# The recurrence-doubling stage of a fused transformer, mixer and expert kernel: four array quadrants with shared q and X banks, and a regrouped state chain

## The reference, cut to what matters

```
def _rwkv7_scan(r, w, k, v, kh, a):
    def step(state, inp):
        r_t, w_t, k_t, v_t, kh_t, a_t = inp
        removed = jnp.einsum('zhvk,zhk->zhv', state, kh_t)
        state = (state * w_t[:, :, None, :] - removed[..., None] * (kh_t * a_t)[:, :, None, :]
                 + v_t[..., None] * k_t[:, :, None, :])
        return state, jnp.einsum('zhvk,zhk->zhv', state, r_t)
    _, y = lax.scan(step, jnp.zeros((z, h, n, n), jnp.float32), seq)
```

## Time and profile before

| | us |
|---|---|
| median of 3 runs | 3404.02 |
| lowest, highest | 3403.05, 3413.53 |
| profiled execution, span | 3408.2 |
| TensorE busy in it | 3111.3 (91%) |
| the changed stage, first F load used to last chain matmul | about 2203 to 2606 of the span |

### The profile page before, as it was taken

The page is one execution under the profiler, slowest core; times in us unless marked ns, Lnnn a source line. Parts: engine busy times, 40 slices in busy tenths (PEclk is TensorE's granted clock), DMA queues, the critical chain, the costliest instruction groups (busy, mean ns, idle before and its releaser), DMA issues. The chain is left out here.

```text
span 3408.2 us, 53296 instructions
## 1 busy us (share of the span) xinstructions
PE 3111.3 (91%) x21800; PEld 2450.2 (72%) x21800; DVE 1944.8 (57%) x2706; ACT 1276.3 (37%) x1607; POOL 903.3 (27%) x468
## 2 busy tenths in 40 slices
PE   7989999998999979999889998389999869999995
PEld 5467888797777767888678776278886358888883
DVE  3656551201433335553399657775644369999995
ACT  2544331222333333222232223222222247777773
POOL 3023434343222214344312200000100014544530
PEclk9989999999999989999999998699999879999997
DMA  3632222321111112222211100501001149999994
GB/s 141 232 115 111 99 93 92 130 99 74 62 50 62 60 48 91 88 97 99 100 74 61 40 17 1 205 3 52 27 27 79 50 187 359 355 373 368 372 371 189
DMA packets 77469, 439.34 MB, mean 129 GB/s; under 512 B 14944, under 2 KB 18016, under 8 KB 28512
## 3 DMA queue, kind: packets, MB, share of 16 engines
q1 hardware_dynamic: 67776, 427.12, 33.4%
q0 software_dynamic: 9504, 9.47, 0.8%
HBM read 421.85 MB, written 39.85 MB: 135 GB/s over the span
## 5 line engine op out<-in xcount | busy, mean ns | idle before, releaser
L77 POOL TENSOR_TENSOR ring_lo<-ring,unit_hi 128x2048 fp32r<-128x2048 f32 x116 | 536.5, 4626 | 1128.0 <-ACT unit_hi L72 1128.0
L130 PE MATMUL wide<-h_hi,unit_hi 128*128 128x512 f32 x1296 | 516.5, 399 | 45.3 <-DVE h_lo L191 23.9
L132 PE MATMUL wide<-h_hi,ring_lo 128*128 128x512 f32 x1296 | 517.0, 399 | 0.0
L131 PE MATMUL wide<-h_lo,unit_hi 128*128 128x512 f32 x1296 | 516.2, 398 | 0.0
L3112 DVE TENSOR_TENSOR ex_w_lo<-ring,ex_w_hi 128x2048 fp32r<-128x2048 f32 x192 | 437.8, 2289 | 46.5 <-ACT ex_w_hi L3062 45.2
L3062 ACT CAST ex_w_hi<-ring 128x2048 fp32r<-128x2048 f32 x192 | 365.7, 1908 | 115.8 <-DMA ring<-in_weights 107.4
L72 ACT CAST unit_hi<-ring 128x2048 fp32r<-128x2048 f32 x116 | 220.5, 1901 | 419.7 <-PE wide L132 418.2
L130 PEld LDWEIGHTS wide<-h_hi,unit_hi 128*128 128x128 f32 x1296 | 250.0, 193 | 117.1 <-POOL ring_lo L77 18.8
L131 PEld LDWEIGHTS wide<-h_lo,unit_hi 128*128 128x128 f32 x1296 | 245.9, 190 | 53.9 <-issue 0.2
L132 PEld LDWEIGHTS wide<-h_hi,ring_lo 128*128 128x128 f32 x1296 | 245.5, 189 | 52.6
L362 DVE TENSOR_TENSOR ffn_hidden_lo<-ffn_whole,ffn_hidden_hi 128x512 f32 (+1 forms) x44 | 201.0, 4569 | 51.3 <-ACT ffn_hidden_hi L337 51.3
(11 more groups left out here) (522 smaller groups left out, 6114.8 us busy)
## 6 DMA issues: line engine op xcount, KB each, us to landing
ring<-in_weights SPq DMA_DIRECT2D x356, 1024.0 KB, 6.1
factors<-rp_out SPq DMA_DIRECT2D x8, 1536.0 KB, 5.5
rw_F<-factors SPq DMA_DIRECT2D x12, 1024.0 KB, 5.3
tail_both<-pair_rows_out SPq DMA_DIRECT2D x4, 1024.0 KB, 7.9
x<-in_x SPq DMA_DIRECT2D x1, 2048.0 KB, 7.6
x_kept<-x SPq DMA_DIRECT2D x1, 2048.0 KB, 12.2
x<-x_kept SPq DMA_DIRECT2D x1, 2048.0 KB, 8.1
x_mixing<-x SPq DMA_DIRECT2D x1, 2048.0 KB, 7.3
```

Source lines behind the costliest of these rows:

```text
L77: pool.tensor_tensor(self.lo[n % RING][:, :], self.ring[n % RING][:, :], self.hi[n % 2][:, :].bitcast(F32), ALU.subtract).then_inc(self.lo ...
L130: pe.matmul(dst, a[0], b[0], start=start, stop=False)
L131: pe.matmul(dst, a[0], b[1], start=False, stop=False)
L132: return pe.matmul(dst, a[1], b[0], start=False, stop=stop)
```

## The change

Both halves of `rwkv_stage` are edited, and the table of masks.

```diff
-        QB, XB = c.bank[0:2], c.bank[2:4]
+        QB, XB, XTB = c.bank[0], c.bank[1], c.bank[2:4]
...
# starts: the output blocks are swapped between the halves
-                            mm = pe.matmul(side[d][h % 2][half[b], m * DH:(m + 1) * DH], F[d][rows, p % 2, m, 0, half[b]],
+                            mm = pe.matmul(side[d][h % 2][half[1 - b], m * DH:(m + 1) * DH], F[d][rows, p % 2, m, 0, half[b]],
...
# pairs
-                    for part in range(2):
-                        for h in (2 * m, 2 * m + 1):
-                            rows = half[h % 2]
-                            ar = F[d][rows, p % 2, m, 0:2, :].rearrange("p a t -> p (a t)")
-                            mm = pe.matmul(side[d][h % 2][:, 2 * P * part:2 * P * (part + 1)], F[d][rows, p % 2, m, 2 + part, :], ar, start=True, stop=True)
+                    for h in (2 * m, 2 * m + 1):
+                        rows = half[h % 2]
+                        for b in both:
+                            pe.matmul(side[d][h % 2][half[1 - b], 0:P], F[d][rows, p % 2, m, 2, half[b]], F[d][rows, p % 2, m, 0, :], start=True, stop=True)
+                    for h in (2 * m, 2 * m + 1):
+                        rows = half[h % 2]
+                        pe.matmul(side[d][h % 2][:, P:2 * P], F[d][rows, p % 2, m, 2, :], F[d][rows, p % 2, m, 1, :], start=True, stop=True)
+                    for h in (2 * m, 2 * m + 1):
+                        rows = half[h % 2]
+                        ar = F[d][rows, p % 2, m, 0:2, :].rearrange("p a t -> p (a t)")
+                        pe.matmul(side[d][h % 2][:, 2 * P:4 * P], F[d][rows, p % 2, m, 3, :], ar, start=True, stop=True).then_inc(pair_done[d], 1)
...
# q_step
-                    if n >= 1:
-                        pe.wait_ge(q_ready[d], n)
+                    if n + d >= 1:
+                        pe.wait_ge(q_ready[1 - d], n + d)
...
-                                mm = pe.matmul(dst[half[b]], G[d][half[b], p % 2, h, half[b]], X[d][half[b], p % 2, h, :], start=True, stop=True)
+                                mm = pe.matmul(dst[half[b]], G[d][half[1 - b], p % 2, h, half[b]], X[d][half[1 - b], p % 2, h, :], start=True, stop=True)
...
# xx_step; earlier_x counts all X copies of earlier slots, both directions
+                    if k < LAST and earlier_x(p, k, d, g) >= 1:
+                        pe.wait_ge(x_taken, earlier_x(p, k, d, g))
...
-                        x, xt = XB[d][:, e * DH:(e + 1) * DH], XB[d][:, (4 + e) * DH:(5 + e) * DH]
+                        x, xt = XB[:, e * DH:(e + 1) * DH], XTB[d][:, e * DH:(e + 1) * DH]
...
-                                mm = pe.matmul(x[half[b]], XT[d][half[b], p % 2, h, :], Q[d][half[b], h, :], start=True, stop=True)
+                                mm = pe.matmul(x[half[1 - b]], XT[d][half[b], p % 2, h, :], Q[d][half[b], h, :], start=True, stop=True)
...
# chain part 0: state first for even m, values first for odd m (part 3 likewise with "corrected", values and U together)
+                            if m % 2 == 0:
+                                state(True)
+                                values(False)
+                            else:
+                                values(True)
+                                mm = state(False)
...
# chain part 2, U
-                            mm = pe.matmul(side[d][h % 2][:, h // 2 * DH:(h // 2 + 1) * DH], full[d][:, h, :], base[d][:, h, :], start=True, stop=True)
+                            for b in both:
+                                mm = pe.matmul(side[d][h % 2][half[b], h // 2 * DH:(h // 2 + 1) * DH], full[d][:, h, half[b]], base[d][:, h, :],
+                                               start=True, stop=True)
...
# VectorE: masks without the repeated half, reads of the other half in L2368, and a signal after the copy of X
-                                          masks.pair[:, d, :].unsqueeze(1).broadcast_to([P, 2, 2 * P]), ALU.mult).then_inc(pair_masked[d], 1)
+                        dve.tensor_tensor(G[d][:, p % 2, h, :], side[d][h % 2], masks.pair[:, d, :], ALU.mult).then_inc(pair_masked[d], 1)
...
-                                            by_four(XB[d], 0))
+                                            by_four(XB, 0)).then_inc(x_taken, 1)
...
-                masks.pair = r_ctx.enter_context(nc.sbuf_tensor("pair_mask", [P, 2, 2 * P], F32))
+                masks.pair = r_ctx.enter_context(nc.sbuf_tensor("pair_mask", [P, 2, 4 * P], F32))
```

More of the change, by code:

```diff
@@ L2255, in chain, with state, values @@
                             ts = slice(m * P, (m + 1) * P)
-                            for a, rows, hs in heads:
-                                pe.matmul(side[d][0][rows, ts], S[d][rows, m, :], F[d][rows, p % 2, m, 0, :], start=True, stop=False)
-                            for a, rows, hs in heads:
-                                mm = pe.matmul(side[d][0][rows, ts], r.vtm[:, t, hs], G[d][:, p % 2, 2 * m + a, 2 * P:3 * P], start=False, stop=True)
+                            def state(first):
+                                for a, rows, hs in heads:
+                                    mm = pe.matmul(side[d][0][rows, ts], S[d][rows, m, :], F[d][rows, p % 2, m, 0, :], start=first, stop=not first)
+                                return mm
+                            def values(first):
+                                for a, rows, hs in heads:
+                                    mm = pe.matmul(side[d][0][rows, ts], r.vtm[:, t, hs], G[d][:, p % 2, 2 * m + a, 2 * P:3 * P], start=first, stop=not first)
+                                return mm
+                            if m % 2 == 0:
[4 more added lines that the diff above has]
+                                mm = state(False)
                         mm.then_inc(baseT_done[d], 1)
@@ L2279, in chain, with state, corrected @@
                                 ts = slice(m * P, (m + 1) * P)
-                                for a, rows, hs in heads:
-                                    pe.matmul(side[d][0][rows, ts], S[d][rows, m, :], F[d][rows, p % 2, m, 1, :], start=True, stop=False)
-                                for a, rows, hs in heads:
-                                    pe.matmul(side[d][0][rows, ts], U[d][:, place(2 * m + a), :], G[d][:, p % 2, 2 * m + a, P:2 * P],
-                                              start=False, stop=False)
-                                for a, rows, hs in heads:
-                                    mm = pe.matmul(side[d][0][rows, ts], r.vtm[:, t, hs], G[d][:, p % 2, 2 * m + a, 3 * P:4 * P],
-                                                   start=False, stop=True)
+                                def state(first):
+                                    for a, rows, hs in heads:
+                                        mm = pe.matmul(side[d][0][rows, ts], S[d][rows, m, :], F[d][rows, p % 2, m, 1, :], start=first, stop=not first)
+                                    return mm
+                                def corrected(first):
+                                    for a, rows, hs in heads:
+                                        pe.matmul(side[d][0][rows, ts], r.vtm[:, t, hs], G[d][:, p % 2, 2 * m + a, 3 * P:4 * P], start=first, stop=False)
+                                    for a, rows, hs in heads:
+                                        mm = pe.matmul(side[d][0][rows, ts], U[d][:, place(2 * m + a), :], G[d][:, p % 2, 2 * m + a, P:2 * P],
+                                                       start=False, stop=not first)
+                                    return mm
+                                if m % 2 == 0:
+                                    state(True)
+                                    mm = corrected(False)
+                                else:
+                                    corrected(True)
+                                    mm = state(False)
                             mm.then_inc(y_done[d], 1)
@@ L2383, in grow @@
                             dve.wait_ge(u_done[d], p)
-                        dve.tensor_copy(full[d][half[a], group(g), half[1 - a]], by_four(XB[d], 4 * DH)[half[a]]).then_inc(x_ready[d], 1)
+                        dve.tensor_copy(full[d][half[a], group(g), half[1 - a]], by_four(XTB[d], 0)[half[a]]).then_inc(x_ready[d], 1)
                 def finish(p, d):
@@ L2476, in carry_q @@
                     rows = slice(0, P) if k < LAST else half[1 - source(d)]
-                    act.copy(Q[d][rows, group(g), :], by_four(QB[d], 0)[rows]).then_inc(q_ready[d], 1)
+                    act.copy(Q[d][rows, group(g), :], by_four(QB, 0)[rows]).then_inc(q_ready[d], 1)
                 def carry_turned(p, d):
```

22 lines of the change are left out of this document (11 added, 11 removed).

## The result

| | before | after |
|---|---|---|
| median (lowest to highest), us | 3403.5 (3401.5 to 3413.5) | 3366.3 (3356.5 to 3374.7) |
| ratio, 95% interval | | 0.9891 (0.9870 to 0.9913) |
| profiled execution, span | 3408.2 | 3372.9 |
| the changed stage in it | 403.6 | 371.0 |
| TensorE idle over 0.25 us with no releaser, in the stage | 4.6 | 11.1 |

The change gains 37 us. That is inside the range, and 11 us short of the point forecast (3355.4). The profiled execution after the change is the slowest of its four, 8 us over their median. The stage is measured from its first `starts` matmul to the first matmul behind the chain (2203.5 to 2607.1 before, 2198.1 to 2569.0 after).

The account below looks back on a forecast made before the run. TensorE was taken to bound the kernel, VectorE period 0. Savings 18.7 + 1.0 + 9.8 + 11.1 + 12.2, less 4.2 lost, make 48.6: span 3408.2 to 3359.6, median 4.2 lower, 3355.4; range 3338 to 3380.

Parts of the forecast that it names:

- supply of instructions and L2368: Rival: TensorE's instruction stalls cost 10 us and VectorE's slower L2368 copy 8, 18 together, giving 3373; chance 0.12.
- holes with "issue" in front: Sign of being wrong: TensorE idle in the stage with nothing shown as awaited, passing 10 us.
- Four quadrants overlap, xx in 0.47: In xx, 32 records in four quadrants take 0.467 us, saving 0.467 a slot; covered slots of periods 1 to 5 save 18.7.
- issue floor: Rival: xx records start more slowly than those of `starts`, so xx takes 0.70 us, giving 3372; chance 0.05.
- The loops: With shared banks, slots without extra wait for copies: q 1.19 us, X 1.29, so a slot goes to 1.29.
- Shape changes: In the chain and at the output, 66 fewer changes of matmul shape at 0.148 us each save 9.8 us.
- U: U's matmuls in two halves take 0.93 us a direction in place of 1.86; 12 times 0.92 saves 11.1.
- Slots 16 to 1: Where VectorE is nearly full beside `pairs`, these slots shrink by 2.0 us a period.
- Slots 12 to 15: These shrink by 1.0 us a period; the two with `starts` go from 1.87 to about 1.45.
- Losses: 4.2 us lost: period 0's waits for xx 2.5, the larger mask table 0.65, first `pairs` at low clock 1.0.
- Supply of instructions: TensorE's stalls without a releaser, with some 8% more instructions coming faster: 0 to +10 us, taken as 0.
- the clock falls: Rival: TensorE's waits in period 0, slots 12 to 1 and period 5's end drop the clock to 0.50, giving 3445; chance 0.03.

Follow-up runs that it names:

- half-instruction pair: q and xx with half as many matmuls of twice the columns, in the changed kernel (ratio 0.9845) and in the kernel before (0.9954).

## Why the prediction was right, and where it was not

The direction and the range came true, and the quadrants overlap as forecast, which is the core of the change. The time, 3366.3, lies 11 us over the point forecast and 7 us under the rival "supply of instructions and L2368" (3373), of which the first half came true and the second did not. Of the prediction's own signs of being wrong one was met: holes with "issue" in front were not to pass 10 us in the stage, and they are 11.1. That the range holds the time all the same is in part luck: it had 8 us of room for L2368, which were not needed, and none for the clock. The steps in their order:

- *Four quadrants overlap, xx in 0.47.* Right: 0.49 with start-up. Slots 4 and 5 were to be 1.66; they are 1.44 and 1.66. Slots 2 to 11 of period 1 went from 27.9 to 21.2, 6.7 against 6.9 forecast, those of period 3 from 35.0 to 27.2, 7.8 against 7.5. The issue floor of the rival did not appear, and the 25 ns of the Trainium skill (TensorE: Matmul & The Clock Gate, Part 1) do not hold across quadrants: L2240 and L2242 start 0.01 us apart, 32 records in 0.49 us are 15 ns each.
- *The loops.* Right and a little too long: a slot without extra is 1.24, forecast 1.29; about 25 of these give 1.2 us more than the sum has. At the last level the loop of q was to be 1.19; at full clock it is 1.19 and 1.20.
- *Shape changes.* Right to the third digit (0.148). *U*: forecast 0.92, measured 0.84 a direction; 12 times, 1.0 us short.
- *Slots 16 to 1.* Right in kind: VectorE 97% busy, no wait on the copies there but through the holes. They went from 23.8 to 21.25 in period 3, 2.5 in place of 2.0. In the four periods from 1 to 4 they shrink by 2.1, 1.6, 2.5 and 1.7, 8 us together as in the sum; with the holes taken out it is 9.4, 1.4 more.
- *Slots 12 to 15.* This step failed. I had the two with `starts` go from 1.87 to about 1.45, "since VectorE has grow, some 0.7, and `finish`, about as long". The rows of slots 14 and 15 above show what I left out: `finish` stands in front of `grow` in VectorE's queue, and with one bank for X the next xx cannot start until that `grow` is through (the waits of 0.68 and 0.42 us for L2412). In period 3 slot 14 takes 2.32 and slot 15, with a hole of 0.91 in it, 3.21, where they were 1.87 and 2.42. Two banks let TensorE run a slot ahead of VectorE; one does not. The half-instruction pair has these four slots 0.07 shorter in period 1 and 0.94, 0.80 and 0.38 longer in 2, 3 and 4, a loss of 2.05 where the sum had a gain of 2.2: 4.3 us. Two holes that are left there (0.50 and 0.47) belong to the supply, so it is 3.3. The wait for VectorE explains it in periods 3 and 4, with output (0.71 and 0.48, 0.70 and 0.48 us before the two xx). In periods 1 and 2 of that run slot 14 takes 1.89 and 1.70, and in slot 15 TensorE waits 0.85 and 0.45 us for the load of F (0.40 and 0 in the kernel before with half the instructions): a wait that the sum had nowhere, and that no run takes apart. In period 5 the same two slots have no `starts` to cover the wait for VectorE: 1.86 and 2.05 where they were 1.40 each and 0.1 was to be saved in each, 1.3 us more.
- *Losses.* Mis-sized. Period 0 lost 2.6 and not 0.5, the start 3.2 and not 1.65: 3.7 us in this pair of profiles. All profiles together shift that: the start is 20.7 us in the mean of the three with the old quadrants and 22.4 in the ten with the new ones, 1.7 more, as forecast; period 0 is 56.2 in the mean of the same three and 59.2 in the six of the new ones that leave it as the change has it, 3.0 more. So the term that was mis-sized is period 0. Four X loops at 0.62 were to be 2.5. VectorE's waits for xx there went from 2.26 to 6.18 us, 3.9 more: 0.57 each at full clock, near my 0.62, but 1.0 at half clock, and 2.40 at the end. For the start no run separates the masks' landing (8.9 us for 512 KB, 7.8 for 256 KB before) from the rest. L2368 did not grow:

```profile
L2405 DVE COPY_PREDICATED rw_XT<-level_mask,rw_G 64x256 f32<-64x256 uint32 x6 | 2.9, 478 | 0.2
```

  478 ns against 526 in the earlier trace rows; 0 was the right one of the two bounds to take.
- *Supply of instructions.* "0 to +10, I take 0" failed. It is 11.1 - 4.6 = 6.5 us, and the sign was in the rows: the one hole in the earlier trace rows lay in a burst of four quadrants, and the change makes every xx such a burst. Growth by 8% in number was the wrong measure. The rate is the right one: the same instructions in 11% less time per slot, across the 74 a microsecond.
- *The clock.* "Granted clock 1.00" failed. The rival "the clock falls" was argued from period 0 alone, where TensorE idle 9.7 of 34 us had kept 1.00; now it is idle 13.4 of 38 and the clock is 0.77. The 50 us at 0.50 were far cheaper than the rival's one us for one: 16 of them lie at the start, which has about 12 in the kernel before too, and 20 in period 0, where VectorE bounds and pays 0.4 us for a copy, more where `turn_hidden` falls into them. The end pays some 4 us by comparison of single profiles. The rival's words "decides from 49 us on" would have made it no gain at all at 50 us; its price was wrong, not its mechanism.

Together: 6.5 (supply) + 4 (clock at the end) + 3.7 (losses) + 3.3 (slots 12 to 15) + 1.3 (the same in period 5) + 1.0 (U) - 1.4 (slots 16 to 1) - 1.2 (loops) = 17.2, and 48.6 - 32.6 = 16.0 are missing in the stage. The terms come from single profiles that differ by 2 or 3 us in a period, so that the sum comes out is no proof of any one of them. The median fell by 37 us and the stage of the profiled executions by 32.6; the stage holds all of the edit, and the rest is the scatter of single executions.

What stays open: what sets the 3.4 us between instruction packets, how much of the 6.5 us of holes is lost to the total, and what the clock costs by itself in period 0 and at the end, since no run changed it alone.

## What to carry to other kernels

Before a matmul is split or made denser, count TensorE's instructions (weight loads too) a microsecond in the new slot, and compare with the rate at which the trace shows holes without a releaser: past it, fewer and wider matmuls are worth more than a better order. When two buffers become one, walk the queue of the engine that frees it, with everything written in front of the freeing instruction: that, and not the length of the copy, is the new loop. Where a wait is taken away, look at what stands behind it in the other engine's queue, and at which clock that will run, before counting the gain.

## What the runs showed of the hardware

- TensorE's instructions come in packets of 16 KB on a DMA queue of their own, some 250 matmuls and weight loads each (250 to 256 between neighbouring holes), never less than 3.31 us apart in any of the thirteen profiles. All 127 holes of TensorE over 0.25 us without a releaser ended 1.09 to 1.61 us after the end of such a packet. Halving the instructions of q and xx at the same columns took 22 us off a stage of 371.
- Matmuls of different quadrants start 0.01 us apart and run ahead of each other: in the changed kernel xx of XT (L2240) begins at 2305.14, and records of the q step ahead of it in the queue (L2217), which use the other two quadrants, still start at 2305.18 to 2305.31.
- The granted clock fell to 0.50 right after holes of 2.22 and 1.21 us, for 3.4 and 10.2 us, and stayed at 1.00 after others of 1.21, 1.99 and 1.33 us. In period 0 it was 0.77 with TensorE busy 24.62 of 38 us; before the change it was 1.00 there with 24.33 of 34. With 8 matmuls of 512 columns in each second slot it was 1.00 in period 0 but for 3.4 us, TensorE busy 31.2 of 41 us. The same 16 transposes took 1.90 us at 1.00 and 3.24 with 2.80 of them at 0.50.
